# One core, a two-block model: small projection columns in four column strips with a fold, decay and beta rows by transposes, one product fewer in an inverse

## The reference

```python
proj = x @ w_in
dn_qkv, dn_z, dn_b, dn_a, sb_qkv, gates = jnp.split(proj, SPLIT_POINTS, axis=-1)   # dn_b, dn_a: 4 columns each
dn_qkv = jax.nn.silu(causal_depthwise_conv(dn_qkv, dn_conv_w))
...
beta = jax.nn.sigmoid(dn_b.astype(jnp.float32)).transpose(0, 2, 1)
g = (-jnp.exp(dn_a_log) * jax.nn.softplus(dn_a + dn_dt_bias)).transpose(0, 2, 1)
...
decay = jnp.cumsum(g.reshape(b, h, n, c), axis=-1)
diff = decay[..., :, None] - decay[..., None, :]
lmask = jnp.where(causal, jnp.exp(jnp.where(causal, diff, 0.0)), 0.0)
a = jnp.where(strict, jnp.einsum("bhnid,bhnjd->bhnij", k_beta, k) * lmask, 0.0)
m = a + jnp.eye(c, dtype=a.dtype)
u = lax.linalg.triangular_solve(m, v_beta, left_side=True, lower=True, unit_diagonal=True)
```

## Time and profile before

| what | us |
|---|---|
| three runs | 1005.76, 1006.05, 1004.15 |
| median | 1005.76 |
| span of the profiled execution, first to last instruction | 1007.2 |
| TensorE matmuls busy in it | 947.1 (94%) |
| VectorE busy | 572.0 (57%) |
| ScalarE busy | 389.0 (39%) |
| GpSimd busy | 32.3 (3%) |

### The profile page before, as it was taken

How to read it: one execution, slowest core, us unless ns; L and a number is a source line. 1 busy time by engine, 2 the same in 40 slices (tenths; PEclk the granted TensorE clock), 3 DMA queues, 4 the chain that set the end, 5 groups by cost and what they waited for, 6 DMA issues and landing times.

```text
span 1007.2 us, 14412 instructions
## 1 busy us (share of the span) xinstructions
PE 947.1 (94%) x5957; PEld 736.1 (73%) x5957; DVE 572.0 (57%) x906; ACT 389.0 (39%) x525; POOL 32.3 (3%) x49
## 2 busy tenths in 40 slices
PE   8999989999999999496989999999999999999997
PEld 7999886677775534142558888888888888888885
DVE  5885473996664102000087657666566786666564
ACT  4554502774252111010056455443343453433341
POOL 1410100003000000000000000000000000000000
PEclk9999999999999999898999999999999999999999
DMA  9824330455789999999896622555454444554421
GB/s 326 251 106 167 113 142 1 143 192 192 309 334 362 420 419 420 419 420 420 347 364 225 222 87 89 177 215 189 167 199 176 167 168 168 195 216 174 167 83 42
DMA packets 67564, 226.39 MB, mean 225 GB/s; under 512 B 4129, under 2 KB 5441, under 8 KB 55857
## 3 DMA queue, kind: packets, MB, share of 16 engines
q1 hardware_dynamic: 65648, 220.24, 58.0%
q0 software_dynamic: 1632, 5.26, 1.6%
q10 hardware_dynamic: 224, 0.07, 0.0%
HBM read 224.50 MB, written 1.05 MB: 224 GB/s over the span
## 4 chain that ended last, share of the span: by engine, by line
PE 78%; DMA 9%; DVE 8%; ACT 2%; issue 2%; SPq 1%; DVEq 0%; ACTq 0%
PE bank L1495 16%; PE bank L1484 11%; PE bank L1485 6%; PE bank L1201 5%; PE bank L747 5%; DMA arena<-in_expert_w_up 4%; PE bank L1349 4%; DMA ring<-in_expert_w_up 3%; PE bank L1069 2%; PE bank L764 2%; PE bank L1111 2%; PE bank L1411 2%; PE bank L1353 2%; PE bank L796 1%; PE bank L1339 1%
## 5 line engine op out<-in xcount | busy, mean ns | idle before, releaser
L2585 DVE TENSOR_TENSOR w_lo<-ring,w_hi 128x2048 fp32r<-128x2048 f32 x76 | 170.5, 2285 | 75.8 <-ACT w_hi L1836 75.7
L1836 ACT ACTIVATE w_hi<-ring 128x2048 fp32r<-128x2048 f32 x76 | 141.3, 1915 | 94.0 <-PE bank L1495 86.3
L1484 PE MATMUL bank<-xT_lo_hi,w_hi 128*128 128x512 f32 x480 | 170.0, 398 | 0.0
L1485 PE MATMUL bank<-xT_lo_hi,w_lo 128*128 128x256 f32 x480 | 134.8, 281 | 0.0
L1484 PEld LDWEIGHTS bank<-xT_lo_hi,w_hi 128*128 128x128 f32 x480 | 90.2, 188 | 22.2
L1495 PE MATMUL bank<-w_hi,hidden_hi 128*128 128x512 f32 x256 | 100.0, 391 | 0.0
L1495 PE MATMUL bank<-w_hi,hidden_lo 128*128 128x512 f32 x256 | 99.8, 390 | 0.0
L1495 PE MATMUL bank<-w_lo,hidden_hi 128*128 128x512 f32 x256 | 99.7, 389 | 0.0
L1485 PEld LDWEIGHTS bank<-xT_lo_hi,w_lo 128*128 128x128 f32 x480 | 90.7, 189 | 0.5
L1201 PE MATMUL bank<-ring,arena 128*32 128x512 f32 x256 | 54.1, 642 | 21.8 <-DMA arena<-in_expert_w_up 21.8
L1934 ACT ACTIVATE arena<-bank 128x256 f32<-128x256 f32 x64 | 21.1, 382 | 109.9 <-PE bank L1485 106.1
(11 more groups left out here) (584 smaller groups left out, 1737.3 us busy)
## 6 DMA issues: line engine op xcount, KB each, us to landing
ring<-in_mlp_w_up SPq DMA_DIRECT2D x32, 1024.0 KB, 6.9
ring<-in_mlp_w_down SPq DMA_DIRECT2D x32, 1024.0 KB, 6.1
ring<-in_w_in SPq DMA_DIRECT2D x22, 1024.0 KB, 8.0
ring<-in_expert_w_gate SPq DMA_DIRECT2D x15, 1024.0 KB, 12.3
ring<-in_expert_w_up SPq DMA_DIRECT2D x15, 1024.0 KB, 15.6
ring<-in_expert_w_down SPq DMA_DIRECT2D x14, 1024.0 KB, 19.9
arena<-in_expert_w_down SPq DMA_DIRECT2D x12, 1024.0 KB, 21.8
ring<-in_attn_w_qkv SPq DMA_DIRECT2D x12, 1024.0 KB, 11.0
```

The source lines that it names most:

```text
L1484: mm(cube(B[4 + c], 2), w_hi[:, at], both_parts(k), start=(k == 0), stop=False)
L1485: last = mm(B[4 + c][:, 0:SEQ], w_lo[:, at], xTH[:, k, 0:SEQ], start=False, stop=(k == KD - 1))
L1836: act(whi[:, n % 2, half], slot(u)[:, half], ACT.Copy).then_inc(S("split_hi"), 1)
L2585: tt(wlo[:, u % SLOTS, half], slot(u)[:, half], f32(whi[:, n % 2, half]), ALU.subtract).then_inc(S("split_lo"), 1)
```

## The change

1. The small columns are made after unit 2 in eight products: `wba`, padded with zeros to 32 columns a slice, is the weight, all 272 tokens move, and slice k lands in column strip k mod 4 of one bank. VectorE copies the result to SBUF (`ba_parts`, `ba_meta`, larger than before), and three products with a 0/1 matrix (`fold`) add the four strips and turn them to tokens by columns. They take `beta_rows`' place in TensorE's queue.
2. The decay sums move ahead of unit 5. VectorE copies them there (`DEC`, semaphore `dec_out`), ahead of unit 6's low part, and spreads `DEC` instead of `G` (`decB`). The decay rows, like the beta rows, are transposes (`tr`) of the spread columns.
3. At level 0 the second product and its subtraction go. GpSimd makes that factor from `AT` with a mask (`level0T`), two multiplications and one subtraction a part; TensorE waits for it (`stacked`) ahead of level 1's second product.

```diff
-SQUARES = ["ident", "upper", "strict", "ones", "lower", "mupper", "mones", "mlower"] + ["neg", "iota", "rep"]
+SQUARES = ["ident", "upper", "strict", "ones", "lower", "mupper", "mones", "mlower"] + ["neg", "iota"]
...
+        "fold": r % 32 == np.arange(8)[None, :], "before": (q % NE < q // NE) & (r >= 0),
...
+    put["level0T"] = (q % 2 == 1) & (row == q - 1)
...
-    gB, bB = AT, XI
+    decB, bB = AT, XI
...
-    wba = cube(sm(KD * 8), KD)
+    wba = cube(arena[:, 18964:18964 + KD * 32], KD)
+    ba_parts, ba_meta = arena[:, 13504:13504 + SEQ], arena[:, 13504 + SEQ:13504 + SEQ + P]
...
+        nc.gpsimd.memset(wba[:, :, :], 0.0).then_inc(S("raw_pad"), 1)
+        pool.wait_ge(S("raw_pad"), 2)
+        pool.dma_start(wba[:, :, 0:8], w_in[:, COL_BA:COL_BA + 8].rearrange("(k p) n -> p k n", p=P)).then_inc(S("wba_in"), 16)
...
+        for i, part in enumerate(PARTS):
+            n = part.stop - part.start
+            pool.wait_ge(S("chunk_dve"), 4 + i)
+            pool.wait_ge(S("stacked"), 2 * i + 2)
+            for rs in HALF_ROWS:
+                last = nc.gpsimd.tensor_tensor(XITc[rs, part, :], AT[rs, part, rs], halves("level0T", n)[rs], ALU.mult)
+            last.then_inc(S("stacked"), 1)
+            pool.wait_ge(S("stacked"), 2 * i + 3)
+            nc.gpsimd.tensor_tensor(XITc[:, part, :], halves("eye2", n), XITc[:, part, :], ALU.subtract).then_inc(S("stacked"), 1)
...
-        def beta_rows():
+        def small_columns():
+
+            pe.wait_ge(S("wba_in"), 16)
+            for half in range(2):
+                for g in range(4):
+                    k = 4 * half + g
+                    last = mm(B[4][32 * g:32 * g + 32, 0:L], wba[:, k, :], xT[:, k, :], start=(half == 0), stop=(half == 1))
+            last.then_inc(S("ba_psum"), 1)
+
+        def fold_small_columns():
 
             pe.wait_ge(S("ba_out"), 2)
-            mm(B[4][:, 32:40], C("rep", META), ba[0:META, 2, :], start=True, stop=True).then_inc(S("ba_psum"), 1)
...
+            for i, part in enumerate((ba_parts[:, 0:P], ba_parts[:, P:SEQ], ba_meta)):
+                last = mm(B[5][:, 8 * i:8 * i + 8], part, C("fold"), start=True, stop=True)
+            last.then_inc(S("ba_psum"), 1)
...
                 if (u, c) == (3, 1):
-                    beta_rows()
+                    fold_small_columns()
...
-                        if u == 2 and p_ > 0 and k % 2 and c < 3:
-                            column = next(between)
...
             split_features(u)
+        small_columns()
...
+        pe.wait_ge(S("g_made"), 1)
+        pe.wait_ge(S("cw_out"), 1)
+        pe.wait_ge(S("ba_out"), 3)
+        mm(B[5][:, 0:8], C("upper"), G[:, 0:8], start=True, stop=True)
...
+        pe.wait_ge(S("g_made"), 3)
+        mm(B[5][:, 32:104], C("ones"), row_sums, start=True, stop=True).then_inc(S("dec_psum"), 1)
         split_tokens(5, [xblk(0), xblk(1)])
...
-                last = mm(dst[:, j * P:(j + 1) * P], gB[:, c, :], rhs_, start=True, stop=True)
+                last = tr(dst[:, j * P:(j + 1) * P], decB[:, c, :], ident)
...
-                last = mm(dst[:, j * P:(j + 1) * P], bB[:, c, :], ident, start=True, stop=True)
+                last = tr(dst[:, j * P:(j + 1) * P], bB[:, c, :], ident)
...
+            if lv == 0:
+                continue
...
+                if lv == 1:
+                    pe.wait_ge(S("stacked"), 2 * i + 4)
...
-        nc.vector.tensor_copy(ba[:, 0:2, :], cube(B[4][:, 0:16], 2)).then_inc(S("ba_out"), 1)
-        nc.vector.tensor_copy(ba[0:META, 2, :], B[4][0:META, 16:24]).then_inc(S("ba_out"), 1)
+        nc.vector.tensor_copy(ba_parts, B[4][:, META:L]).then_inc(S("ba_out"), 1)
+        nc.vector.tensor_copy(cube(ba_meta, 4), B[4][:, 0:32].unsqueeze(1).broadcast_to([P, 4, 32])).then_inc(S("ba_out"), 1)
...
+        for c in range(NM):
+            last = ts(decB[:, c, :], C("ones"), DEC[:, c:c + 1], None, ALU.mult)
+        last.then_inc(S("g_made"), 1)
+        first_low(6)
...
+                if lv == 0:
+                    tt(XIc[:, part, :], halves("eye2", n), TMc[:, part, :], ALU.subtract).then_inc(S("inv_step"), 1)
+                    continue
```

More of the change, by code:

```diff
@@ L60 @@
 IN_0 = P - META
-SQUARES = ["ident", "upper", "strict", "ones", "lower", "mupper", "mones", "mlower"] + ["neg", "iota", "rep"]
+SQUARES = ["ident", "upper", "strict", "ones", "lower", "mupper", "mones", "mlower"] + ["neg", "iota"]
 VECTORS = ["emb_g", "emb_b", "mix0", "mix1", "mlp0", "mlp1", "ln2_g", "ln2_b", "ln1_g", "ln1_b"]
-HALVES = ["eye2"] + [f"level{i}" for i in range(LEVELS - 1)]
-SMALL = {"hmask": DN_H, "idx4": NG, "desc4": NG, "desc8": NE, "freq": HALF, "eps5": 1, "eps5a": 1, "eps6": 1, "one": 1, "zero": 1}
+HALVES = ["eye2", "level0T"] + [f"level{i}" for i in range(LEVELS - 1)]
+SMALL = {"hmask": DN_H, "idx4": NG, "desc4": NG, "desc8": NE, "freq": HALF, "eps5": 1, "eps5a": 1, "eps6": 1, "one": 1, "zero": 1, "fold": 8}
 def const_layout():
@@ L806, in _ @@
             split_features(u)
+        pe.wait_ge(S("g_made"), 1)
+        pe.wait_ge(S("cw_out"), 1)
+        pe.wait_ge(S("ba_out"), 3)
+        mm(B[5][:, 0:8], C("upper"), G[:, 0:8], start=True, stop=True)
+        mm(B[5][:, 8:9], C("mupper"), G[:, 8:9], start=True, stop=True)
+        mm(B[5][:, 16:24], C("ones"), G[:, 0:8], start=True, stop=True)
+        mm(B[5][:, 24:25], C("mones"), G[:, 8:9], start=True, stop=True)
+        pe.wait_ge(S("g_made"), 3)
+        mm(B[5][:, 32:104], C("ones"), row_sums, start=True, stop=True).then_inc(S("dec_psum"), 1)
         split_tokens(5, [xblk(0), xblk(1)])
@@ L818, in _ @@
         split_tokens(6, [xblk(0)])
[L819 to L827, removed]
+        pe.wait_ge(S("g_made"), 4)
         pe.wait_ge(S("ba_out"), 3)
         for i, part in enumerate(PARTS):
-            rhs_ = C("upper") if i < 2 else C("mupper")
             dst = B[4] if i == 0 else B[6] if i == 1 else B[7]
             for j, c in enumerate(range(part.start, part.stop)):
-                last = mm(dst[:, j * P:(j + 1) * P], gB[:, c, :], rhs_, start=True, stop=True)
+                last = tr(dst[:, j * P:(j + 1) * P], decB[:, c, :], ident)
             last.then_inc(S("row_psum"), 1)
@@ L882, in _ @@
                 last.then_inc(S("inv_ax"), 1)
+            if lv == 0:
+                continue
             for i, part in enumerate(level_parts(lv)):
                 pe.wait_ge(S("inv_masked"), inverse_count(lv, i))
-                if lv and with_rows(lv, i):
+                if lv == 1:
+                    pe.wait_ge(S("stacked"), 2 * i + 4)
+                if with_rows(lv, i):
                     for j, c in enumerate(range(part.start, part.stop)):
@@ L891, in _ @@
                         xax = XAX_BANK[i][rs, j * HW:(j + 1) * HW]
-                        last = mm(xax, TMc[rs, c, :], XITc[rs, c, :], start=True, stop=True) if lv else mm(xax, TMc[rs, c, :], C("ident")[rs, rs], start=True, stop=True)
+                        last = mm(xax, TMc[rs, c, :], XITc[rs, c, :], start=True, stop=True)
                 last.then_inc(S("inv_xax"), 1)
@@ L2081, in _ @@
         dve.nop().then_inc(S("g_made"), 1)
-        for dst, src in ((gB, G), (bB, BE)):
-            for c in range(NM):
-                last = ts(dst[:, c, :], C("ones"), src[:, c:c + 1], None, ALU.mult)
+        for c in range(NM):
+            last = ts(bB[:, c, :], C("ones"), BE[:, c:c + 1], None, ALU.mult)
         last.then_inc(S("g_made"), 1)
@@ L2092, in _ @@
         first_low(5)
+        dve.wait_ge(S("dec_psum"), 1)
+        line(nc.vector.tensor_copy(DEC, B[5][:, 0:NM]))
+        line(nc.vector.tensor_copy(DL, B[5][:, 16:16 + NM]))
+        nc.vector.tensor_copy(row_1, B[5][:, 32:68])
+        line(tt(row_0, B[5][:, 68:104], rbias, ALU.add))
+        tt(KF, DL, DEC, ALU.subtract).then_inc(S("dec_out"), 1)
+        for c in range(NM):
+            last = ts(decB[:, c, :], C("ones"), DEC[:, c:c + 1], None, ALU.mult)
+        last.then_inc(S("g_made"), 1)
         first_low(6)
```

31 lines of the change are left out of this document (7 added, 24 removed).

## The result

The changed kernel takes 1009.39 us (median of 7 runs, 1008.45 to 1012.71), the kernel before 1005.76 us beside it (7 runs, 1003.88 to 1006.62): a ratio of 1.0041, 95% interval 1.0027 to 1.0055. By the medians it is 3.6 us slower; I had said 1.1 us slower, with 1009.0 us as the upper end.

The account below looks back on a forecast made before the run. The prediction took TensorE (78% of the chain) and, in the projections, also VectorE as near their limit. Its terms 0 + 1.5 - 0.5 + 0.1 = +1.1 us on the median 1005.76 gave 1006.9 us, range 1003.4 to 1009.0.

Parts of the forecast that it names:

- Step 1: Small columns: gain 0, 0.4 us either way; the fold waits for VectorE's copies and starts at about 65.3 us.
- Step 2: TensorE's new wait before the fold lowers its clock, slowing the work behind it: +1.5 us, lower end 0.
- Step 3: Decay sums moved earlier, 1.07 us more there; row stage by transposes, 1.55 less: net -0.5 us.
- Step 4: Inverse's first level: 0.65 us saved, one meeting of VectorE and GpSimd paid; +0.1 us, ends -0.65 and +1.5.
- my 0.72: Inverse's first level: the most that one meeting of a VectorE operation with GpSimd's instructions costs, in us.
- my sum: Whole kernel: the four steps together, +1.1 us; chance of this forecast 0.55.
- They cost nothing: Three loads in GpSimd's queue, waiting behind its nine instructions in the inverse until near 132 us: price 0.
- A: Rival at the fold: the clock holds through TensorE's wait; -0.4 us, 1005.4 us, chance 0.17.
- B: Rival in the inverse's first level: GpSimd meets all three VectorE operations; +1.5 us there, 1008.3 us, chance 0.16.
- C: Rival: TensorE's freed small-column time reaches the end, clock holds, inverse keeps its gain; -6.4 us, 999.4 us, chance 0.12.

Follow-up runs that it names:

- Experiment 8: The changed kernel measured and profiled again, nothing altered; ratio 1.0044 to the kernel before.
- experiment 1: The kernel before with only the small-column strips and the fold added; ratio 1.0012 to the kernel before, 1.2 us slower.
- Experiment 4: The changed kernel with five unread products of a constant ahead of the fold's wait; ratio 1.0019 to the kernel before.
- Experiment 2: The kernel before with only the decay sums moved and the decay and beta rows made by transposes; ratio 1.0012 (0.9999 to 1.0026).
- experiment 3: The kernel before with only the inverse's first level changed, GpSimd making the transposed factor; ratio 1.0004 to the kernel before.
- 7: experiment 5 with GpSimd's three parameter loads ahead of its nine instructions and VectorE's two multiplications behind the inverse; ratio 0.9980 to the kernel before.
- 11: experiment 5 with only VectorE's two multiplications moved behind the inverse; ratio 0.9986 to the kernel before.
- experiment 5: The changed kernel with the fold ahead of unit 3's last group, VectorE and ScalarE reordered so nobody waits for it; 1005.84 us, ratio 1.0004.
- experiment 9: The kernel of 7 with VectorE's router row sums in its wait for ScalarE and beta copies behind the decay copies; 998.45 us, ratio 0.9934.
- experiment 10: experiment 5 with only GpSimd's three parameter loads moved ahead of its nine instructions; ratio 1.0002 to the kernel before.

## Why the prediction was wrong

**Step 1, right.** The freed time is lost before the fold: fold at 65.36 us (I said 65.3), wait 5.12 us (4.9 at most), strips 1.06 us, four at once. Experiment 8 shows that the time of TensorE's arrival does not matter.

**Step 2, the clock, is the step that failed.** The mechanism was right, the size was not. I priced it at 1.5 us, 1.7 at most, from one line's products after waits. With the longer fold (66.66 against the 66.00 us that I had forecast) the loss at the end of unit 4 is 3.32 us in the first profile, 90.15 - 86.83; in experiment 8 the sums start at 89.53 us, 2.70 late; in experiment 1 it is 1.98. Counted from its fall the clock is low for 10.2 us in the first profile and for 6.8 in experiments 1 and 8. What lies inside the wait (3.1, 2.6 and 0.7 us) costs nothing; of the rest (7.2, 4.2 and 6.1) a little under half is lost. So a shorter wait is not a cheaper one: experiment 8 waited 2 us less than experiment 1 and lost 0.7 more. Experiment 4 gives it all back by keeping TensorE at work.

**Step 3, right in the profile.** The sums take 1.03 us ahead of unit 5 (1.07). Unit 6's first tile starts at 109.59 us, 4.49 later than before (105.10), its second 2.97 later: 1.52 us come back in the row stage (1.55). Net -0.49. Experiment 2's times don't confirm it.

**Step 4, right up to level 1, wrong behind it.** GpSimd and VectorE meet at the two multiplications: 1.83 us instead of 1.28, 0.55 against my 0.72; the masks stay at 0.89 us. By the Trainium skill's rule (SBUF — State Buffer, Who interferes with whom), that a VectorE instruction with two SBUF inputs contends with a GpSimd instruction that reads SBUF, and that the ports they share are an exclusive lock, the two multiplications and the subtractions would all wait. The trace agrees that they do, but not at my price of 0.72 us each: the multiplications take 0.78 and 1.12 us instead of 0.68, the three subtractions 0.04 to 0.12 us more each. GpSimd waits too: its pair L660 takes 1.68 us beside the multiplications and 1.32 beside VectorE's L2150, which reads one input from PSUM. So level 1 starts 0.15 us earlier relative to level 0. But my sum ended there. The second product that was removed had kept TensorE at work between two short waits (0.39 us here and 0.27 behind it):

```profile
131.44 1.26 PE L892 MATMUL bank<-cst,arena 64*64 64x64 f32 x36 [0.39 <-DVE arena L2146]
```

Without it there is one wait of 1.78 us, the clock falls, and from level 0 to the last level's products (154.76 against 150.56 us) the shift grows by 4.20 - 2.97 = 1.23 us (0.75 in experiment 3). I had priced a wait's clock in step 2 and did not ask for it here.

**What the steps add up to.** In the profile the changed kernel is 3.32 us late at the end of unit 4, 2.97 behind the row stage, 2.82 at level 1, 4.20 at the last level and 5.60 at the 96 products, where my sum had 1.1. Step 2 is 1.8 us of that miss. Another 2.8 us come behind level 1, from two falls of the clock that my sum put at nothing: 1.4 us from the one behind level 0, and 1.4 from the one at 158 us (in experiment 8 the shift grows by as much there, from 6.53 to 7.91 us). The first of these two has its cause shown, by experiments 3, 7 and 11; the second has not.

**The loads of GpSimd's queue.** "They cost nothing" is not a safe statement. With the loads behind the nine instructions, three of six profiles (experiments 4, 5 and 8, but not the first one, 3 and 11) have an "issue" wait of 1.2 to 1.8 us in the inverse; with the loads first (7, 9, 10) none of three has. In these three the wait stands inside a group of 16 rows of one line (behind the third or the 13th), where the program waits for nothing. Instructions come by DMA too: the transfers of experiment 4 list one block of an instruction queue between 139 and 141.5 us, while the parameters hold 54% of the engines. The Trainium skill (Runtime: NRT & Kernel Launch, Instruction fetch mechanics) says that a sequencer fetches its instructions in blocks by a DMA queue of its own, mostly hidden. That this block was TensorE's, and late, is argued, not shown; three of six against none of three is no proof either, and experiment 10, which moves the loads alone, has the time of experiment 5.

**The rivals.** A is out: the clock fell. B is out by the sign that I gave: level 1 starts 3.05 us behind level 0, not over 0.5 us later than before (3.20). All three operations meet GpSimd, but together they lose about the price of one meeting. C did not come, by the cause that I gave, VectorE's queue. But I wrote that it needs the convolutions to end 5 us sooner. It needed the fold to stand later, and experiment 9 gets 6.6 us from that, with the waits at the first level and at unit 5 taken away too. In its profile the 96 products start at 251.83 us, 6.36 earlier than before, which is about C's sum.

**The span.** I called the profiled execution 1.4 us slower than the median, from its span of 1007.2 us. A span is shorter than the time of its run (1008.3 beside 1010.13 us, 1005.4 beside 1007.61), so that execution was slower than I took it for. The forecast does not use it.

**Open.** The falls at 119 and 158 us, which only the changed kernel's profiles show; why the clock stayed low for 10.2 us in the first profile and for 6.8 in the two others; experiment 2's times; the experts' stage.

## What to carry to other kernels

Time taken from a bounding engine counts only if its next consumer is not waiting for another engine's queue; look for the first later instruction that waits, and move that, before making the work smaller. A wait newly opened on TensorE can have a second price behind it, about half of the work done at the lower clock (2.0 to 3.3 us at the fold, 0.9 to 1.4 us in the inverse), also where the removed work was only a filler between two short waits. After each wait taken away look for the next: here three went (at the fold, at the first level, at unit 5), and most of the gain came with the last.

## What the hardware showed that I had not expected

The price of a clock fall is not constant: 4.2 us of work at the low clock behind a wait of 5.02 us, 6.1 behind 3.09, 7.2 behind 5.12. A wait of 1.78 or 1.79 us behind level 0 went with a clock of 0.50, in it or up to 1.3 us behind it, in all five profiles where nothing else was changed there (the changed kernel twice, experiments 3, 4, 5) and in 10; one of 0.87 us (7, 9, 11) did not. Four strips of 32 columns run at once: their 16 passes of 272 columns take 1.06 us, where 16 fp32 passes of 272 columns at full width, in the sums of squares of the changed kernel, take 3.83:

```profile
102.20 3.83 PE L835 MATMUL bank<-arena,cst 128*128 128x272 f32 x16
```
